# Sample rows of the attention projections as plain fp32 products on four column groups

## The chip, the cores and the metric

The kernel runs on one core of one Trainium2 chip. The metric is the device time of one execution in microseconds; the median of three runs before the change is 1368.88 us. The engines are TensorE (matrix products, PE in the rows, its weight loads PEld), VectorE (DVE), ScalarE (ACT), GpSimd (POOL) and SyncE (SP), which here only starts transfers. All run their own instruction stream and meet through semaphores.

## What is computed

Two layers of an encoder, for 512 prompt rows and 32 sample rows of width 1024. Layer 0 mixes tokens by pooling, layer 1 by banded attention with 16 heads of 64; after each comes a mixture of 32 experts of which each row uses two. The change touches one product of layer 1:

```
h   = rms_norm(x, norm_mix[1])                      # 512 + 32 rows
qkv = einsum('bld,de->ble', h, w_qkv)               # 1024 -> 3072
q   = rms_norm(qkv[:, :, 0], q_gain)                # per head
k   = rms_norm(qkv[:, :, 1], k_gain)
v   = qkv[:, :, 2]
```

The same product is taken for the prompt rows and for the sample rows.

## The kernel before

**Tiles.** The rows lie in five tiles (NT = 5): four of 128 prompt rows and one of SS = 32 sample rows. The contraction over 1024 channels goes in KT = 8 chunks of 128. The 3072 output columns go in QKV_PIECES = 6 pieces of 512: pieces 0 and 1 are q, 2 and 3 are k, 4 and 5 are v. A piece of the weights (2 MB) lies in one of the SLOTS = 3 slots of `ring`; piece j lies in slot j modulo 3. The output of tile i of piece j is bank (5 j + i) modulo 6 of PSUM.

**Split products.** A product of fp32 precision is made of three in the rounded format fp32r. ScalarE copies a quarter of a piece (two chunks) to `w_hi` rounded (line 877), VectorE takes the rest to `w_lo` (line 1268); each such copy waits on `quarters_used`, that is until TensorE has read that quarter of the piece before. The transposed rows are split likewise, `hT_hi` and `hT_lo`. `token_quarter` issues, for a prompt tile and a quarter, 2 chunks x 3 products (lines 1740 to 1742). For the sample rows `hT_sample` holds, for each chunk, 32 columns of the high part and 32 of the rest side by side, so `sample_quarter` issues 2 chunks x 2 products of 64 stationary columns (lines 2140 and 2141). Its output has 64 partitions: rows of the high part in 0 to 31 and rows of the rest in 32 to 63. ScalarE copies the upper half to `stacked` (`stack_out`, line 1118) and VectorE adds it to the lower (`add_stack`, line 1630).

**Order of a piece.** In `token_product` each of the first three quarters runs tiles 0 to 3 and then the sample rows, and then `between` transposes two finished tiles of the q or k piece before (`qk_transposes`, lines 2118 and 2120); the last quarter runs the sample rows first and then tiles 0 to 3. Each engine's order is written out by hand. ScalarE: three quarters of the next piece's split, `stack_out`, squares and roots of the five tiles (lines 1087 and 1094), or the v copies (line 1106), and then the last quarter of the split. VectorE: the same quarters, `add_stack`, head sums (line 1608), reciprocals and scalings (line 1621), last quarter. POOL multiplies by the gains (line 801) and stores k. TensorE takes a bank again when `raw_free` finds the tile six places back scaled or copied. Piece 0 has an order of its own, `first_product`, where tiles 0 to 2 run alone and tile 3 together with the sample rows.

**Around it.** SyncE loads a piece (line 683) when the piece three before is split, `split_lo`. After the last piece TensorE goes on with attention: scores (line 2241), to which VectorE adds a table of biases (line 1669) from slot 2 of the ring. POOL loads the tables (line 823) when the last piece is split, masks them (line 830), and reloads a slot when it has been read. Later the sample rows of the attention output's product run in `sample_product` (line 2309): eight fp32 products of 32 stationary columns for each half of the columns, chunk k on column group k modulo 4, and are added up by a product with `fold` (line 2316).

Of the kernel before, what the change touches and what calls it, by code (L numbers as in the profile page):

```python
# [81 lines left out]
def encoder(nc, A, O, cols):  # L82
# [32 lines left out]
    with ctx:  # L115
# [3 lines left out]
        def sem(name):  # L119
            return ctx.enter_context(nc.semaphore(name))  # L120
# [16 lines left out]
        hT_hi = nc.alloc_sbuf_tensor_at("hT_hi", [P, KT, S], F32R, offset=third_at)  # L137
        hT_lo = nc.alloc_sbuf_tensor_at("hT_lo", [P, KT, S], F32R, offset=third_at + 4 * KT * S)

        hT_sample = nc.alloc_sbuf_tensor_at("hT_sample", [P, KT, 2 * SS], F32R, offset=third_at + 8 * KT * S)  # L140
        xT_at = -(-nc.sbuf_base // 32) * 32
        xT = sb("xT", [P, 2, KT * BLK])
        hidT = sb("hidT", [P, FT * BLK])
# [129 lines left out]
        wo_all = pair[:, :, :].rearrange("p a n -> p (a n)").rearrange("p (k d) -> p k d", k=KT)  # L273
        wo_stacked = [gain[:, hf * 512:(hf + 1) * 512] for hf in range(2)]
        xT_flat = xT[:, :, :].rearrange("p u n -> p (u n)")
        stacked = xT_flat[0:SS, 0:512]
        rw_groups = xT_flat[:, 0:KT * NG]
        rw_experts = xT_flat[:, KT * NG:KT * NR].rearrange("p (g n) -> p g n", g=NG)
        early_rows = third_pair[:, 1, :]
# [105 lines left out]
        raw_ps = sem("raw_ps")  # L385
        stack_ps = sem("stack_ps")
        stack_sb = sem("stack_sb")
        sample_sum = sem("sample_sum")
        q_sq = sem("q_sq")
        q_ssq = sem("q_ssq")  # L390
# [155 lines left out]
        def _(sp):  # L546
# [32 lines left out]
            for l in range(L):  # L579
# [88 lines left out]
                if l == 0:  # L668

                    sp.wait_ge(y_ps, NEXP - 2)  # L670
                    sp.dma_start(att_gain, A["norm_mix"][1:2, :].broadcast_to((P, D))).then_inc(gain_in, 16)
                    for j in range(QKV_PIECES):
                        if j < 2:

                            sp.wait_ge(gu_ps, NEXP - 1)
                        elif j == 2:

                            sp.wait_ge(y_ps, NEXP - 1)
                        else:

                            sp.wait_ge(split_lo, QUARTERS * (j - 2))
                        to = ring[:, j % SLOTS, :].rearrange("p (k e) -> p k e", k=KT)
                        sp.dma_start(to, wqkv[:, :, j * 512:(j + 1) * 512]).then_inc(piece_in[j % SLOTS], 16)

                    half = slice(512, 1024)
                    for i in range(NT):

                        sp.wait_ge(v_sb, NT + i + 1)
                        dst = (O[5][0, 0].rearrange("t h d -> t (h d)")[i * P:(i + 1) * P, half] if i < NT - 1
                               else O[7][0, 0].rearrange("t h d -> t (h d)")[:, half])  # L690
                        sp.dma_start(dst, v_nat[0:ROWS[i], i, half]).then_inc(v_second_out, 16)
# [14 lines left out]
        def _(pool):  # L706
# [125 lines left out]
            store_first_v()  # L832

            pool.wait_ge(split_lo, QUARTERS * QKV_PIECES)
            for u in range(BIASES):
                load_bias(u)
            for u in range(BIASES):
# [15 lines left out]
        def _(act):  # L853
# [26 lines left out]
            def transpose_out(ph, i):  # L880

                n = ROWS[i]
                act.wait_ge(hT_ps, (ph - 1) * NT + i + 1)
                b = transposed_bank(ph, i)
                act.activation(hT_hi[:, :, i * P:i * P + n] if i < NT - 1 else hT_sample[:, :, 0:SS],
                               ps[:, b:b + 2, :].rearrange("p b (c t) -> p (b c) t", c=4)[:, :, 0:n],
                               ACT.Copy).then_inc(hT_hi_sb, 1)

# [220 lines left out]
            def stack_out(j):  # L1109

                if j == 0:
                    act.wait_ge(rw_set, 2)
                else:

                    act.wait_ge(sample_sum, j)
                act.wait_ge(stack_ps, j + 1)
                m = j * NT + NT - 1
                act.activation(stacked, ps[SS:2 * SS, m % RAW_BANKS, :], ACT.Copy).then_inc(stack_sb, 1)

            EARLY_HEADS = 2  # L1120

            for j in range(QKV_PIECES):
# [20 lines left out]
                if j < QKV_PIECES - 2:  # L1143
                    done = EARLY_HEADS if j == 0 else 0
                    squares(j * NT + done)
                    for i in range(done, NT):
                        if i + 1 < NT:
                            squares(j * NT + i + 1)
                        head_roots(j * NT + i)
                else:  # L1150
                    for i in range(NT):
                        v_out_of_ps((j - QKV_PIECES + 2) * NT + i)
                if j + 1 < QKV_PIECES:
                    split_att(j + 1, [QUARTERS - 1])

# [87 lines left out]
        def _(dve):  # L1243
# [27 lines left out]
            def transpose_out(ph, i):  # L1271

                n = ROWS[i]
                b = transposed_bank(ph, i)
                hi, lo = ((hT_hi[:, :, tok(i)], hT_lo[:, :, tok(i)]) if i < NT - 1 else
                          (hT_sample[:, :, 0:SS], hT_sample[:, :, SS:2 * SS]))
                dve.wait_ge(hT_hi_sb, (ph - 1) * NT + i + 1)
                V.tensor_tensor(lo, ps[:, b:b + 2, :].rearrange("p b (c t) -> p (b c) t", c=4)[:, :, 0:n],  # L1278
                                f32(hi), ALU.subtract).then_inc(hT_sb, 1)


            V.memset(spare[:, 0:1], 1.0).then_inc(spare_set, 1)
# [328 lines left out]
            def scale_heads(m):  # L1611
# [4 lines left out]
                if m >= NT:  # L1616

                    dve.wait_ge(qkT_ps, m - NT + 1)
                    if m >= 3 * NT:
# [3 lines left out]
                                bc(qstat[0:n, c + 16:c + 24], (n, 512 // HD, HD), 2),  # L1623
                                ALU.mult).then_inc(q_scaled, 1)

            def add_stack(piece):

                out = ps[0:SS, (piece * NT + NT - 1) % RAW_BANKS, :]
                dve.wait_ge(stack_sb, piece + 1)
# [4 lines left out]
            for j in range(QKV_PIECES):  # L1634

                if j == 0:
                    head_sums(0)
                    head_sums(1)
                    scale_heads(0)
                    scale_heads(1)  # L1640
                if j + 1 < QKV_PIECES:
                    split_att(j + 1, range(QUARTERS - 1))
                add_stack(j)
                if j < QKV_PIECES - 2:
                    done = EARLY_HEADS if j == 0 else 0
                    head_sums(j * NT + done)
                    for i in range(done, NT):
                        if i + 1 < NT:
                            head_sums(j * NT + i + 1)
                        scale_heads(j * NT + i)  # L1650
                if j + 1 < QKV_PIECES:
                    split_att(j + 1, [QUARTERS - 1])

# [76 lines left out]
        def _(pe):  # L1730
# [399 lines left out]
                                         w_hi[:, q, at], w_lo[:, q, at], k == 0, k == KT - 1)  # L2130
                return last

            def sample_quarter(m, q):

                for kk in range(KT // QUARTERS):
                    k = q * KT // QUARTERS + kk
                    at = slice(kk * 512, (kk + 1) * 512)
                    rows = hT_sample[:, k, :]
                    out = ps[0:2 * SS, m % RAW_BANKS, :]
                    mm(out, rows, w_hi[:, q, at], start=(k == 0), stop=False)  # L2140
                    last = mm(out, rows, w_lo[:, q, at], start=False, stop=(k == KT - 1))
                return last

            def first_product():

# [5 lines left out]
                for i in range(early):  # L2151
# [10 lines left out]
                            transposes(2, i + 2)  # L2162
                    last.then_inc(raw_ps, 1)
                sample = NT - 1
                for q in range(QUARTERS - 1):
                    if q == 0:
                        pe.wait_ge(hT_sb, NT + early + 1)
                    token_quarter(early, early, q)
                    if q == 0:
                        pe.wait_ge(z_sb[0], finished(4))  # L2170
                        pe.wait_ge(hT_sb, NT + sample + 1)
                    sample_quarter(sample, q).then_inc(quarters_used, 1)
                sample_quarter(sample, QUARTERS - 1).then_inc(stack_ps, 1)
                token_quarter(early, early, QUARTERS - 1).then_inc(quarters_used, 1)

            def token_product(piece, between):
# [3 lines left out]
                for q in range(QUARTERS - 1):  # L2180

                    pe.wait_ge(split_lo, QUARTERS * piece + q + 1)
                    for i in range(NT):
                        if q == 0:
                            raw_free(m0 + i)
                        if i < sample:
                            token_quarter(m0 + i, i, q)
                        else:
                            sample_quarter(m0 + i, q).then_inc(quarters_used, 1)
                    if between is not None:  # L2190
                        between(q)
# [120 lines left out]

            def sample_fold(hf):

                pe.wait_ge(stack_sb, QKV_PIECES + hf + 1)
# [82 lines left out]
```

## Time and profile before

| | |
|---|---|
| timed runs | 1363.88, 1368.88, 1369.61 us (median 1368.88) |
| span of the profiled execution | 1356.4 us from first to last instruction |
| the profiled execution's own time | not listed beside the three timed runs; its span is 12.5 us below their median |
| TensorE busy in the span | 1309.7 us, 97% |
| VectorE, ScalarE, POOL busy | 571.6, 299.8, 122.4 us |
| projections | 539 to 712.5 us after the span's start |

Times in the rows are microseconds from the span's start, unless marked ns. A product is shown as one record for each pass; an fp32 product leaves two, a rounded one leaves one. Products are pipelined, so a record lasts longer than the distance to the next one's start. The chain of waits goes back from the last instruction to what released each step.

### The profile page before, as it was taken

The page shows a single profiled execution, that of the slowest core. Times are in us where ns is not written, and L with a number is a line of the kernel's source. Part 1 is how long each engine was busy: PE and PEld are TensorE (multiplying, and loading weights), DVE is VectorE, ACT ScalarE, POOL GpSimd, SP SyncE. Part 2 cuts the span into 40 slices and gives each one's busy share as a digit, 9 for nine tenths or more (in the row PEclk, how much of TensorE's full clock was granted, in tenths as well). Part 3 has the DMA queues.
Part 4 walks back from the last instruction along what each step waited for, and adds up shares of the span by engine and source line. Part 5 has one row for each costly group of instructions (what it writes and reads, how often), then busy time and mean ns, then how long its engine had stood idle before and what let it go on. Part 6 is the DMA issues. An engine that isn't in the chain of part 4 may idle for free.

```text
span 1356.4 us, 19908 instructions
## 1 busy us (share of the span) xinstructions
PE 1309.7 (97%) x7552; PEld 659.5 (49%) x7552; DVE 571.6 (42%) x1057; ACT 299.8 (22%) x638; POOL 122.4 (9%) x196
## 2 busy tenths in 40 slices
PE   9999999999999999999999999999999999999998
PEld 7743344334343334788876544643344334343333
DVE  4643334333343334743418553443334433333433
ACT  4211111111111114433326443211111111111111
POOL 1010000000000001222222220010000000000000
PEclk9999999999999999999999999999999999999999
DMA  9899999999999999221038323899999999999996
GB/s 362 329 358 421 426 427 428 426 429 427 427 429 426 427 424 367 78 85 73 34 120 284 91 44 128 363 355 419 427 427 427 426 429 427 427 428 428 427 424 249
DMA packets 53504, 459.61 MB, mean 339 GB/s; under 512 B 8077, under 2 KB 9357, under 8 KB 28106
## 3 DMA queue, kind: packets, MB, share of 16 engines
q1 hardware_dynamic: 41246, 426.46, 75.3%
q0 software_dynamic: 9552, 23.94, 5.6%
q10 hardware_dynamic: 2652, 8.45, 1.7%
q8 instruction: 39, 0.64, 0.2%
q14 instruction: 15, 0.12, 0.0%
HBM read 455.42 MB, written 11.26 MB: 344 GB/s over the span
## 4 chain that ended last, share of the span: by engine, by line
PE 91%; issue 3%; DVE 3%; DMA 2%; ACT 1%; SPq 0%; POOL 0%; DVEq 0%; POOLq 0%
PE ps L1900 33%; PE ps L1931 11%; PE ps L1909 9%; PE ps L1910 8%; PE ps L2331 4%; PE ps L1740 3%; PE ps L1742 3%; PE ps L1741 3%; PE ps L1892 2%; PE ps L1824 1%; PE ps L1812 1%; PE ps L1918 1%; PE ps L2265 1%; PE ps L2281 1%; DMA ring<-in_rel_bias_reversed 1%
## 5 line engine op out<-in xcount | busy, mean ns | idle before, releaser
L1500 DVE TENSOR_TENSOR x<-x,ps 128x1024 f32<-128x1024 f32 (+1 forms) x150 | 177.7, 1216 | 222.1 <-PE ps L1931 221.0
L1900 PE MATMUL ps<-ring,xT 128*64 128x512 f32 x352 | 160.8, 606 | 8.2 <-issue 6.6
L1900 PE MATMUL ps<-pair,xT 128*64 128x512 f32 x352 | 160.7, 606 | 7.5 <-issue 7.5
L1514 DVE SCALAR_TENSOR_TENSOR nat<-nat,slot_gate,ps 64x256 f32<-64x256 f32 x128 | 86.1, 673 | 191.8 <-ACT nat L1012 163.6
L1901 PE MATMUL ps<-ring,xT 128*64 128x512 f32 x352 | 160.9, 606 | 0.0
L1901 PE MATMUL ps<-pair,xT 128*64 128x512 f32 x352 | 160.8, 607 | 0.0
L1931 PE MATMUL ps<-y_parts,hot 64*128 64x512 f32 (+1 forms) x1200 | 160.2, 401 | 0.0
L1900 PE MATMUL ps<-third_pair,xT 128*64 128x512 f32 x320 | 143.6, 597 | 7.2 <-issue 7.2
L1910 PE MATMUL ps<-qk,hidT 128*64 128x512 f32 x320 | 144.9, 595 | 0.0
L1909 PE MATMUL ps<-qk,hidT 128*64 128x512 f32 x320 | 144.7, 595 | 0.0
L1901 PE MATMUL ps<-third_pair,xT 128*64 128x512 f32 x320 | 143.8, 597 | 0.0
L1012 ACT ACTIVATE nat<-ps 64x512 f32<-64x512 f32 x62 | 36.9, 595 | 482.8 <-PE ps L1901 482.8
L1931 PEld LDWEIGHTS ps<-y_parts,hot 64*128 64x128 f32 (+1 forms) x1200 | 98.6, 171 | 71.7 <-issue 48.5
L1477 DVE TENSOR_TENSOR y_parts<-ps,y_parts 128x512 fp32r<-128x512 f32 x60 | 41.5, 692 | 133.3 <-ACT y_parts L997 133.3
L1900 PEld LDWEIGHTS ps<-ring,xT 128*64 128x64 f32 x352 | 46.3, 139 | 96.7 <-issue 95.6
L1900 PEld LDWEIGHTS ps<-pair,xT 128*64 128x64 f32 x352 | 46.2, 138 | 96.2 <-issue 95.0
L1900 PEld LDWEIGHTS ps<-third_pair,xT 128*64 128x64 f32 x320 | 41.4, 137 | 86.0 <-issue 85.0
L1909 PE MATMUL ps<-ring,hidT 128*64 128x512 f32 x176 | 79.7, 595 | 1.6 <-ACT xT L978 1.6
L1910 PE MATMUL ps<-ring,hidT 128*64 128x512 f32 x176 | 79.7, 596 | 0.0
L997 ACT ACTIVATE y_parts<-ps 128x512 fp32r<-128x512 f32 x60 | 35.8, 597 | 192.2 <-PE ps L1910 192.2
L1740 PE MATMUL ps<-w_hi,hT_hi 128*128 128x512 f32 x192 | 76.2, 397 | 0.7 <-DVE hT_lo L1278 0.7
L1742 PE MATMUL ps<-w_lo,hT_hi 128*128 128x512 f32 x192 | 74.9, 390 | 0.0
(243 smaller groups left out, 1784.4 us busy)
## 6 DMA issues: line engine op xcount, KB each, us to landing
qk<-in_moe_w_down SPq DMA_DIRECT2D x40, 2048.0 KB, 29.2
ring<-in_moe_w_down SPq DMA_DIRECT2D x22, 2048.0 KB, 26.8
ring<-in_moe_w_gate SPq DMA_DIRECT2D x20, 2048.0 KB, 24.3
ring<-in_moe_w_up SPq DMA_DIRECT2D x20, 2048.0 KB, 29.1
third_pair<-in_moe_w_gate SPq DMA_DIRECT2D x20, 2048.0 KB, 23.2
third_pair<-in_moe_w_up SPq DMA_DIRECT2D x20, 2048.0 KB, 27.9
pair<-in_moe_w_gate SPq DMA_DIRECT2D x18, 2048.0 KB, 25.9
pair<-in_moe_w_up SPq DMA_DIRECT2D x18, 2048.0 KB, 30.3
```

What stands on the lines that cost most here:

```text
L1477: V.tensor_tensor(y_rest[v], ps[:, bank, :], f32(y_high[v]), ALU.subtract).then_inc(y_lo[l], 1)
L1500: return V.tensor_tensor(x[0:n, i, :], x[0:n, i, :], ps[0:n, bank:bank + 2, :].rearrange("p b c -> p (b c)"), ALU.add)
L1514: last = V.scalar_tensor_tensor(out=out[u * BLK:(u + 1) * BLK, :].rearrange("s (k p) -> s k p", k=n), in0=act_rows[:, u * n:(u + 1) * n, : ...
L1740: mm(out, x_hi, w_h, start=start, stop=False)
L1741: mm(out, x_lo, w_h, start=False, stop=False)
L1742: return mm(out, x_hi, w_l, start=False, stop=stop)
L1900: mm(ps[BLK:P, GU_BANK, :], rows, gate[:, at], start=(k == 0), stop=(k == KT - 1))
L1901: last = mm(ps[0:BLK, GU_BANK, :], rows, up[:, at], start=(k == 0), stop=(k == KT - 1))
L1909: mm(ps[0:BLK, bank, :], rows, slot[:, at:at + 512], start=(k == 0), stop=(k == FT - 1))
L1910: last = mm(ps[BLK:P, bank, :], rows, slot[:, at + 512:at + D], start=(k == 0), stop=(k == FT - 1))
L1931: last = mm(ps[0:n, bank + hf, :], (hot[v] if by is None else by)[slots, tok(i)], part[slots, :], start=first and at == 0, stop=final and ...
L2331: last = mm(ps[:, WO_BANK, :], oT[:, k, tok(i)], wo_all[:, k, hf * 512:(hf + 1) * 512], start=(k == 0), stop=(k == KT - 1))
```

## The change

The sample rows are no longer split. `hT_sample` keeps, at the same place in memory, the transposed rows in plain fp32; ScalarE copies four chunks and VectorE the other four. For each piece `sample_rows` issues eight fp32 products of 32 stationary columns against the unsplit weights in the ring, chunk k on column group k modulo 4, so four partial sums over two chunks each lie in partitions 0 to 127 of the bank. They are added in two levels: ScalarE copies partitions 64 to 127 to `stacked_odd` and VectorE adds them to 0 to 63; then ScalarE copies 32 to 63 to `stacked` and VectorE adds them to 0 to 31.

The eight products run in one go behind the third quarter's tokens (behind the first in the last piece; between the third and the last of tile 3 in piece 0). `quarters_used` is now raised by the token products. Since the ring is read by the sample product too, SyncE's later piece loads and POOL's bias loads wait for `stack_ps` as well.

```diff
-        hT_sample = nc.alloc_sbuf_tensor_at("hT_sample", [P, KT, 2 * SS], F32R, offset=third_at + 8 * KT * S)
+        hT_sample = third_pair[:, 1, :][:, 2 * KT * S - KT * T:].rearrange("p (k t) -> p k t", k=KT)
...
-        stacked = xT_flat[0:SS, 0:512]
+        stacked_odd = xT_flat[0:2 * SS, 0:512]
+        stacked = xT_flat[0:SS, 512:1024]
...
                             sp.wait_ge(split_lo, QUARTERS * (j - 2))
+                            sp.wait_ge(stack_ps, j - 2)
...
             pool.wait_ge(split_lo, QUARTERS * QKV_PIECES)
+            pool.wait_ge(stack_ps, QKV_PIECES)
...
+                if i == NT - 1:
+                    act.activation(hT_sample[:, 0:KT // 2, 0:SS],
+                                   ps[:, b, :].rearrange("p (c t) -> p c t", c=4)[:, :, 0:n],
+                                   ACT.Copy).then_inc(hT_hi_sb, 1)
+                    return
...
                 act.wait_ge(stack_ps, j + 1)
+                m = j * NT + NT - 1
+                act.activation(stacked_odd, ps[2 * SS:P, m % RAW_BANKS, :], ACT.Copy).then_inc(stack_sb, 1)
+
+            def half_out(j):
+
+                act.wait_ge(sample_half, j + 1)
                 m = j * NT + NT - 1
                 act.activation(stacked, ps[SS:2 * SS, m % RAW_BANKS, :], ACT.Copy).then_inc(stack_sb, 1)
...
                     squares(j * NT + done)
+                    half_out(j)
...
                         v_out_of_ps((j - QKV_PIECES + 2) * NT + i)
+                        if i == 0:
+                            half_out(j)
...
+                if i == NT - 1:
+                    dve.wait_ge(hT_ps, (ph - 1) * NT + i + 1)
+                    V.tensor_copy(hT_sample[:, KT // 2:KT, 0:SS],
+                                  ps[:, b + 1, :].rearrange("p (c t) -> p c t", c=4)[:, :, 0:n]).then_inc(hT_sb, 1)
+                    return
...
+            def add_odd(piece):
+
+                out = ps[0:2 * SS, (piece * NT + NT - 1) % RAW_BANKS, :]
+                dve.wait_ge(stack_sb, 2 * piece + 1)
+                V.tensor_tensor(out, out, stacked_odd, ALU.add).then_inc(sample_half, 1)
...
-                add_stack(j)
+                add_odd(j)
                 if j < QKV_PIECES - 2:
                     done = EARLY_HEADS if j == 0 else 0
                     head_sums(j * NT + done)
+                    add_stack(j)
...
+                else:
+                    add_stack(j)
...
-            def sample_quarter(m, q):
-
-                for kk in range(KT // QUARTERS):
-                    k = q * KT // QUARTERS + kk
-                    at = slice(kk * 512, (kk + 1) * 512)
-                    rows = hT_sample[:, k, :]
-                    out = ps[0:2 * SS, m % RAW_BANKS, :]
-                    mm(out, rows, w_hi[:, q, at], start=(k == 0), stop=False)
-                    last = mm(out, rows, w_lo[:, q, at], start=False, stop=(k == KT - 1))
-                return last
+            def sample_rows(piece):
+
+                for k in range(KT):
+                    at = k % HEADS_A_GROUP * SS
+                    last = mm(ps[at:at + SS, (piece * NT + NT - 1) % RAW_BANKS, :], hT_sample[:, k, 0:SS],
+                              ring[:, piece % SLOTS, k * 512:(k + 1) * 512],
+                              start=(k < HEADS_A_GROUP), stop=(k >= KT - HEADS_A_GROUP))
+                last.then_inc(stack_ps, 1)
...
                 for q in range(QUARTERS - 1):
-                    if q == 0:
-                        pe.wait_ge(hT_sb, NT + early + 1)
-                    token_quarter(early, early, q)
-                    if q == 0:
-                        pe.wait_ge(z_sb[0], finished(4))
-                        pe.wait_ge(hT_sb, NT + sample + 1)
-                    sample_quarter(sample, q).then_inc(quarters_used, 1)
-                sample_quarter(sample, QUARTERS - 1).then_inc(stack_ps, 1)
+                    token_quarter(early, early, q).then_inc(quarters_used, 1)
+                pe.wait_ge(z_sb[0], finished(4))
+                pe.wait_ge(hT_sb, NT + sample + 1)
+                pe.wait_ge(hT_hi_sb, NT + sample + 1)
+                sample_rows(0)
                 token_quarter(early, early, QUARTERS - 1).then_inc(quarters_used, 1)
...
-                    for i in range(NT):
+                    for i in range(sample):
                         if q == 0:
                             raw_free(m0 + i)
-                        if i < sample:
-                            token_quarter(m0 + i, i, q)
-                        else:
-                            sample_quarter(m0 + i, q).then_inc(quarters_used, 1)
+                        last = token_quarter(m0 + i, i, q)
+                    last.then_inc(quarters_used, 1)
+                    if q == (0 if piece == QKV_PIECES - 1 else QUARTERS - 2):
+                        raw_free(m0 + sample)
+                        sample_rows(piece)
                     if between is not None:
                         between(q)
                 q = QUARTERS - 1
                 pe.wait_ge(split_lo, QUARTERS * piece + q + 1)
-                sample_quarter(m0 + sample, q).then_inc(stack_ps, 1)
```

## Rows read from the trace of the kernel before

**Rows 1.** The page: busy us, share of the span and records of each engine.
```profile
PE 1309.7 (97%) x7552; PEld 659.5 (49%) x7552; DVE 571.6 (42%) x1057; ACT 299.8 (22%) x638; POOL 122.4 (9%) x196
```

**Rows 2.** Stretches: start:end, length, busy us by engine, granted clock, DMA share, GB/s.
```profile
570.10:600.00 29.90, 29.90 (x152) 24.29 (x151) 13.23 (x21) 11.09 (x21) 4.92 (x4) 1.00 0.20 71
...
687.00:712.50 25.50, 25.50 (x114) 19.87 (x113) 1.91 (x2) 4.53 (x8) 6.50 (x13) 1.00 0.43 136
...
892.00:1350.00 458.00, 445.28 (x2568) 182.88 (x2570) 171.86 (x255) 65.39 (x128) 18.08 (x30) 0.99 0.98 413
```

**Rows 3.** Chain of waits, 535 to 720 us, by line.
```profile
by line: PE ps L1740 23.7%; PE ps L1742 23.4%; PE ps L1741 23.3%; PE ps L2140 6.3%; PE ps L2141 6.0%; PE ps L2118 4.9%; DMA ring<-in_rel_bias_reversed 3.7%; PE ps L2120 2.3%; PE ps L1758 2.0%; DVE hT_lo L1278 1.3%; ACT hT_hi L885 1.1%; issu
```

**Rows 4.** Waits, 535 to 720 us: who, for whom, total, times, longest.
```profile
ACT w_hi L877 <- PE ps L2141: 56.8, 15, 5.9
```

**Rows 5.** Products of line 2140: ns min/median/max, first and last start, shapes.
```profile
L2140 PE MATMUL ps<-w_hi,hT_sample x48: 387/397/443, 562.1 to 706.4; 128*64 128x512 f32 x48
```

**Rows 6.** Timeline, piece 1, second quarter: start, length, instruction.
```profile
583.30 0.39 PE L1742 MATMUL ps<-w_lo,hT_hi 128*128 128x512 f32 x1
...
583.53 0.40 PE L2140 MATMUL ps<-w_hi,hT_sample 128*64 128x512 f32 x1
...
584.45 1.95 PE L2118 MATMUL ps<-cst,nat 128*128 128x128 f32 x16
```

**Rows 7.** Chain behind 32-row transposes, piece 2.
```profile
624.07 0.37 PE ps L2140
```

**Rows 8.** Line 2309: weight loads (ns min/median/max), then timeline of products.
```profile
L2309 PEld LDWEIGHTS ps<-pair,third_pair x32: 106/110/110, 855.4 to 858.1; 128*32 128x32 f32 x32
...
855.48 3.64 PE L2309 MATMUL ps<-pair,third_pair 128*32 128x512 f32 x32 [0.87 <-DVE x L1697]
...
858.48 0.64 PE L2309 MATMUL ps<-pair,third_pair 128*32 128x512 f32 x4
...
859.05 1.16 PE L1758 MATMUL ps<-cst,third_pair 128*128 128x128 f32 x8
```

**Rows 9.** Timeline, expert stage: from rounded products into two column groups.
```profile
957.12 2.10 PE L1931 MATMUL ps<-y_parts,hot 64*128 64x512 f32 x16
959.15 0.64 PE L1900 MATMUL ps<-third_pair,xT 128*64 128x512 f32 x1
...
959.63 0.59 PE L1900 MATMUL ps<-third_pair,xT 128*64 128x512 f32 x1
```

**Rows 10.** Timeline, end of piece 0 (first row) and of piece 1.
```profile
572.09 0.69 DVE L1621 TENSOR_TENSOR nat<-ps,nat 128x512 f32<-128x512 f32 x1
...
594.71 0.39 PE L1740 MATMUL ps<-w_hi,hT_hi 128*128 128x512 f32 x1
...
594.97 0.59 ACT L1118 ACTIVATE xT<-ps 32x512 f32<-32x512 f32 x1 [0.86 <-PE ps L2141]
...
595.59 0.69 DVE L1630 TENSOR_TENSOR ps<-ps,xT 32x512 f32<-32x512 f32 x1 [0.39 <-ACT xT L1118]
...
598.29 0.69 DVE L1608 TENSOR_REDUCE nat<-nat 128x8 f32<-128x512 f32 x1 [0.68 <-ACT nat L1087]
...
601.98 0.69 DVE L1621 TENSOR_TENSOR nat<-ps,nat 128x512 f32<-128x512 f32 x1
```

**Rows 11.** Loads of the weight pieces, and ScalarE's first use of piece 3.
```profile
DMA to landing us min/median/max: 8.4/13.1/23.3
...
606.80 1.06 ACT L877 ACTIVATE w_hi<-ring 128x1024 fp32r<-128x1024 f32 x1 [2.26 <-PE ps L2141]
```

**Rows 12.** Timeline of POOL before attention.
```profile
689.72 2.18 POOL L823 DMA_DIRECT2D ring<-in_rel_bias_reversed  x3 [1.64 <-DVE w_lo L1268]
...
697.24 0.20 POOL L830 MEMSET ring<- 64x128 f32 x1 [1.06 <-DMA ring<-in_rel_bias_reversed]
```

**Rows 13.** Chain of waits where attention starts.
```profile
712.51 1.09 PE ps L2241 x8
...
715.35 6.89 DMA ring<-in_rel_bias_reversed
```

More of the change, by code:

```diff
@@ L138, in encoder @@
         hT_lo = nc.alloc_sbuf_tensor_at("hT_lo", [P, KT, S], F32R, offset=third_at + 4 * KT * S)
-        hT_sample = nc.alloc_sbuf_tensor_at("hT_sample", [P, KT, 2 * SS], F32R, offset=third_at + 8 * KT * S)
+        hT_sample = third_pair[:, 1, :][:, 2 * KT * S - KT * T:].rearrange("p (k t) -> p k t", k=KT)
+        assert hT_sample.shape[2] == 2 * SS
         xT_at = -(-nc.sbuf_base // 32) * 32
@@ L387, in encoder @@
         stack_sb = sem("stack_sb")
+        sample_half = sem("sample_half")
         sample_sum = sem("sample_sum")
@@ L884, in transpose_out @@
                 b = transposed_bank(ph, i)
-                act.activation(hT_hi[:, :, i * P:i * P + n] if i < NT - 1 else hT_sample[:, :, 0:SS],
+                if i == NT - 1:
[3 more added lines that the diff above has]
+                    return
+                act.activation(hT_hi[:, :, i * P:i * P + n],
                                ps[:, b:b + 2, :].rearrange("p b (c t) -> p (b c) t", c=4)[:, :, 0:n],
@@ L1274, in transpose_out @@
                 b = transposed_bank(ph, i)
-                hi, lo = ((hT_hi[:, :, tok(i)], hT_lo[:, :, tok(i)]) if i < NT - 1 else
-                          (hT_sample[:, :, 0:SS], hT_sample[:, :, SS:2 * SS]))
+                if i == NT - 1:
[3 more added lines that the diff above has]
+                    return
                 dve.wait_ge(hT_hi_sb, (ph - 1) * NT + i + 1)
-                V.tensor_tensor(lo, ps[:, b:b + 2, :].rearrange("p b (c t) -> p (b c) t", c=4)[:, :, 0:n],
-                                f32(hi), ALU.subtract).then_inc(hT_sb, 1)
+                V.tensor_tensor(hT_lo[:, :, tok(i)], ps[:, b:b + 2, :].rearrange("p b (c t) -> p (b c) t", c=4)[:, :, 0:n],
+                                f32(hT_hi[:, :, tok(i)]), ALU.subtract).then_inc(hT_sb, 1)
             V.memset(spare[:, 0:1], 1.0).then_inc(spare_set, 1)
@@ L1624, in scale_heads @@
                                 ALU.mult).then_inc(q_scaled, 1)
+            def add_odd(piece):
+                out = ps[0:2 * SS, (piece * NT + NT - 1) % RAW_BANKS, :]
+                dve.wait_ge(stack_sb, 2 * piece + 1)
+                V.tensor_tensor(out, out, stacked_odd, ALU.add).then_inc(sample_half, 1)
             def add_stack(piece):
                 out = ps[0:SS, (piece * NT + NT - 1) % RAW_BANKS, :]
-                dve.wait_ge(stack_sb, piece + 1)
+                dve.wait_ge(stack_sb, 2 * piece + 2)
                 V.tensor_tensor(out, out, stacked, ALU.add).then_inc(sample_sum, 1)
@@ L2164, in first_product @@
                 sample = NT - 1
+                pe.wait_ge(hT_sb, NT + early + 1)
                 for q in range(QUARTERS - 1):
-                    if q == 0:
-                        pe.wait_ge(hT_sb, NT + early + 1)
-                    token_quarter(early, early, q)
-                    if q == 0:
-                        pe.wait_ge(z_sb[0], finished(4))
-                        pe.wait_ge(hT_sb, NT + sample + 1)
-                    sample_quarter(sample, q).then_inc(quarters_used, 1)
-                sample_quarter(sample, QUARTERS - 1).then_inc(stack_ps, 1)
+                    token_quarter(early, early, q).then_inc(quarters_used, 1)
[3 more added lines that the diff above has]
+                sample_rows(0)
                 token_quarter(early, early, QUARTERS - 1).then_inc(quarters_used, 1)
@@ L2313, in sample_fold @@
             def sample_fold(hf):
-                pe.wait_ge(stack_sb, QKV_PIECES + hf + 1)
+                pe.wait_ge(stack_sb, 2 * QKV_PIECES + hf + 1)
                 mm(ps[0:SS, WO_SAMPLE_BANKS[hf], :], const("fold"), wo_stacked[hf], start=True,
```

## The prediction

> **What bounds the kernel now.** I read the page's busy shares and slices first. TensorE is busy 97% of the span, VectorE 42%, ScalarE 22% [rows 1]. The change lies between the two expert stages, so the next views are of that part. Seen by stretches, the projections run from 539 to 712.5 us, and from 562.1 us on TensorE is busy in all of each stretch, 29.90 of 29.90 us in piece 1 and 25.50 of 25.50 in piece 5 (first and last of five stretches alike), at clock 1.00, which is the level of 2.4 GHz, while the DMA share is 0.20 and 0.43 [rows 2]. The chain of waits over 535 to 720 us runs through TensorE products nearly throughout, and the sample rows' two lines hold 6.3% and 6.0% of it, 22.8 us of 185 [rows 3]. ScalarE waited 56.8 us there for the last sample product of a quarter [rows 4]: it follows TensorE with room, and VectorE follows it. So a microsecond taken from TensorE in this stage comes off the end, as long as no wait takes its place.
>
> **What is removed.** Sixteen rounded products per piece (8 chunks by two weight parts), 96 in all: 48 on line 2140 [rows 5] and as many on 2141. Each lasts about 0.40 us but the next starts 0.23 us later: four from 583.53, and the following transposes start at 584.45, 0.92 us for four [rows 6]. 96 x 0.23 = 22.1 us. The chain's 22.8 us holds in addition a first product of 0.37 instead of 0.23 us behind each block of 32-row transposes [rows 7]. In the new order a token product stands there and should pay the same 0.14 us (five times 0.7 us), so I don't count it.
>
> **What is added on TensorE.** Eight fp32 products of 32 columns per piece, 48 in all. The same pattern is already in the kernel: the attention output's sample rows (line 2309) run sixteen such products, each of which leaves two records, 32 in all [rows 8]. They start at 855.48 us, the last four records start together at 858.48, and the next work starts at 859.05. Eight waves of four: seven intervals in 3.00 us, 0.43 us each. A piece needs 8 products x 2 records / 4 = 4 waves, 4 x 0.43 = 1.71 us. Two costs come with it. Leaving the groups: 859.05 - 858.48 = 0.57 us instead of 0.43, so 0.14. Entering them from a full stream of products: line 2309 starts after a wait and can't show it. The nearest rows are the expert stage, where 16 rounded products on two halves of the array (8 pairs, at 0.23 us 1.84 us) start at 957.12 and two column groups start at 959.15, 2.03 us later, with 0.48 us to the next pair instead of 0.43 [rows 9]: 0.19 + 0.05 = 0.24 at most. The switch from full width to 64 columns at 583.53 costs nothing [rows 6]. I take 0.2, nearer to the group case. So 1.71 + 0.14 + 0.2 = 2.05 us a piece, 12.3 us for six.
> The bounds: no switching cost, 1.71 x 6 = 10.3 us; at the other end four weight loads of 0.11 us (the median of line 2309's loads is 110 ns) one after the other before the groups run, 0.44 + 0.05 + 0.14 + 1.71 = 2.34 us, 14.0 us for six [rows 8, 9].
> The Trainium skill, "TensorE: Matmul & The Clock Gate", Part 3, "Measured speedup vs the span model", gives 3.07x for four tiles packed by rows and 2.38x for three by columns, not the full 4x and 3x. By 3.07x, eight products that take 6.83 us in sequence would take 2.22 us, six pieces 13.3 us, and the gain would be 8.8 us; the waves of 0.43 us in line 2309 don't show that loss, but its ends might be where it sits.
>
> **Sum.** 22.1 - 12.3 = 9.8 us less TensorE work on the path; by the bounds 22.1 - 14.0 = 8.1 to 22.1 - 10.3 = 11.8.
>
> **The longer addition.** Each piece now needs two evictions and two additions for the sample rows instead of one of each. ScalarE gains a copy of 0.6 us and VectorE an addition of 0.7 us per piece (over 32 partitions they take 0.59 and 0.69 us, and VectorE takes the same 0.69 over 128, so I give 64 partitions the same) [rows 10]. In 29.90 us of a piece VectorE is busy 13.23 and ScalarE 11.09 us [rows 2]: throughput is no matter. Order is. Queued behind the first new addition on VectorE are the head sums and scalings; TensorE's next piece waits for them before it reuses a bank. Tile 3's first quarter in the next piece needs tile 2 scaled. Piece 1's last quarter starts at 594.71 and holds 24 products, so it ends at about 600.2, and tile 3 is due three tiles (18 products, 4.1 us) later, 604.3; tile 2's scaling starts at 601.98 and lasts 0.69: 1.6 us of room [rows 10]. The first addition falls before the last quarter, since the sample product moves ahead of it, and its transposes and 5.5 us of tokens cover it. The second falls between two head sums where VectorE waited 0.68 us for ScalarE [rows 10], and it is 0.69 long: about 0.1 us later, hidden. In piece 0 the products 2 and 3 come closer: tile 2's scaling ends at 572.8 [rows 10] and is due 4.1 us behind 570.1, at 574.2 [rows 2]; both move up by some 2 us, the scaling perhaps by 0.4 us less, still 0.8 us of room. If that cover went, each addition would cost up to its 0.7 us, in five pieces 3.5 us. The copies of the sample's transposed rows were 0.38 us on ScalarE and then 0.42 on VectorE, and now run beside each other; TensorE wasn't waiting for them, so nothing.
>
> **The new waits.** SyncE may load piece j only after sample product j-3. Piece 3's load, before released by the split of piece 0, now goes at about 567 (570.1, where piece 0's products ended, less the 1.4 us of its last quarter and the 1.6 us gained); piece 4's at about 590, piece 5's near 618. The longest such load took 23.3 us to land [rows 11]. ScalarE took piece 3 up behind piece 2's first quarter, at 606.80 [rows 11], so now at about 603.5, and pieces 4 and 5 one piece of about 28 us later each: 13 us of room or more. Behind the wait in SyncE's queue are only the later pieces and then the second value half's stores, which wait for later work anyway. POOL's bias loads wait for the last sample product. They were issued at 689.72, 22.8 us ahead of the end of the projections, and their last mask was written at 697.24, 7.5 us later [rows 12]. The last piece does its sample product after its first quarter, 5.5 + 2.05 us from its start, and the piece lasts 25.5 - 1.6 us: the loads go 16.4 us ahead of the end and are ready 8.9 us ahead. The cached values and four sample tables queued behind them end 3 us later. Hidden; without the cover, each microsecond would delay the first scores.
>
> **What follows.** Attention starts right behind the last projection product: scores at 712.51, then VectorE, then a bias load of 6.89 us that is issued only once a slot is read [rows 13]. All of it, and layer 1's expert loads, are released by progress, not by a clock, so 9.8 us move to the end: span 1356.4 -> 1346.6. The runs' median is 1368.88, 12.5 us above this span; I take that distance as fixed: 1368.9 - 9.8 = 1359.1 us.
>
> **The rivals.**
> (a) The sum holds, 8.1 to 11.8 us gained, 1357.1 to 1360.8. For it: TensorE without a gap in the stage. Chance 0.67.
> (b) More is lost at the edges of the groups, or the additions make the next piece wait by their 0.7 us: gain 9.8 - 3.5 = 6.3, or down to 3 with both, 1362 to 1366. Against it: the room worked out above; for it: 0.8 us in piece 0 is thin and the entry isn't shown. Chance 0.17.
> (c) The gain is spent at the border to attention: the bias loads go 16.4 instead of 22.8 us ahead and would have to take over 16 us (7.5 shown), or layer 1's transfers, at a DMA share of 0.98 in its stage [rows 2], don't start sooner. The loads start on attention's progress, which speaks against it. Gain under 3 us, 1366 to 1370. Chance 0.06.
> (d) Slower: products that read the raw weights from the ring while ScalarE, VectorE and DMA use it don't run four at a time. In sequence a piece costs 16 x 0.43 = 6.8 us instead of 3.68, six pieces 18.9 us more: 1387.8. It decides from the point where fewer than 1.9 groups run at once. Line 2309 speaks against it. Chance 0.03.
> (e) More than the sum: entries cost nothing and the 0.14 us after the transposes goes too, gain 12 to 14 us, 1355 to 1357. Chance 0.07.
>
> **Numbers.** A measurement of this kernel tells about 0.5% (6.8 us) from no change: faster than 1362.0. (a) and (e) and a third of (b), with something off for the scatter of runs (1363.88 to 1369.61 before), give 0.77 faster; (c) and most of (b) 0.18 the same; (d) and mishaps 0.05 slower. The range reaches over (e) and into (b): 1354 to 1364.5.
>
> **What the changed profile would show.** TensorE still busy in every stretch of the projections; 96 records on the new sample line, 16 a piece within about 1.9 us of starts, in waves of four 0.43 us apart; no wait of a token product for VectorE's scaling or for the split weights; scores starting some 9.8 us sooner and everything after at the old distances. Records that start one by one would prove (d); a TensorE wait for the scaling (b); a late first bias mask (c).

## The result, and the profile after

The changed kernel took 1351.97 us (median of four executions, 1349.69 to 1354.55), beside 1366.38 us (1360.69 to 1369.61) for the kernel before: ratio 0.9898, 95% interval 0.9876 to 0.9920. The forecast was 1359.1 us, 1354.0 to 1364.5: faster, as forecast, but 14.4 us instead of 9.8, and below the range. Two later sets with more executions, each with both kernels on one chip, put the ratio at 0.9925 (0.9899 to 0.9950) and 0.9930 (0.9904 to 0.9956), with medians of 1353.43 against 1363.01 us and 1353.20 against 1361.88. One of the changed kernel's 22 executions in the three sets fell in a slow state and took 2608.72 us, at a mean granted clock of 1.00; why is not known, and it is left out of every figure here.

The page's first line answers to [rows 1]:

```profile
PE 1302.5 (96%) x7552; PEld 651.2 (48%) x7552; DVE 577.8 (43%) x1063; ACT 303.7 (22%) x644; POOL 122.8 (9%) x196
```

TensorE gave up 7.2 us of busy time, VectorE and ScalarE took on 6 instructions each. The next fence has the changed kernel in stretches, as [rows 2] but for TensorE alone: start:end, length, busy us and records, granted clock, DMA share, GB/s. The borders are the same events in each kernel: the first expert transposes, the first projection product, the first scores, the first sample product of line 2309 (2336 after), layer 1's first gathered transposes, the end.

```profile
74.20:540.30 466.10, 451.10 (x2603) 0.99 1.00 420
540.30:704.90 164.60, 163.49 (x832) 0.99 0.24 81
704.90:848.50 143.60, 135.82 (x941) 1.00 0.44 138
848.50:895.00 46.50, 44.81 (x279) 1.00 0.94 377
895.00:1351.30 456.30, 438.58 (x2515) 0.99 0.97 411
```

The same borders in the kernel before, first profile:

```profile
74.70:539.10 464.40, 450.57 (x2603) 0.99 1.01 421
539.10:712.40 173.30, 172.23 (x832) 1.00 0.23 78
712.40:855.50 143.10, 135.89 (x945) 1.00 0.44 138
855.50:901.90 46.40, 44.78 (x279) 1.00 0.94 377
901.90:1356.40 454.50, 437.37 (x2515) 0.99 0.98 413
```

Read down the lengths: the projections went from 173.3 to 164.6 us, and the other stretches differ by 0.1 to 1.8 us, all against the changed kernel. The spans are only 5.1 us apart while the timed medians are 14.4 apart. The changed kernel's profiled execution took 1353.18 us at a span of 1351.3, 1.9 us more than its span; with that, the profile of before belongs to an execution of about 1358.3 us, below all four timed ones and 8 us below their median of 1366.38. And the 164.6 us hold something that isn't the change, in this fence of 4 us stretches of the changed kernel:

```profile
556.00:560.00 4.00, 2.93 (x20) 1.00 0.00 0
560.00:564.00 4.00, 4.00 (x14) 0.59 0.45 131
564.00:568.00 4.00, 4.00 (x21) 0.99 0.00 0
```

TensorE had waited 1.1 us for the rest of tile 3's rows (busy 2.93 of 4.00), then the granted clock fell to its lower level of 1.2 GHz for part of 560 to 564 us: 4 x 0.41 = 1.6 us of work lost, which leaves 163.0 us. The kernel before has the same wait at the same place and did not lose its clock there in either profile.

The new products, in piece 0 and in piece 2 (timeline of the changed kernel; line 2168 is `sample_rows`, 1771 to 1773 the token products, 2149 the transposes):

```profile
567.45 0.39 PE L1773 MATMUL ps<-w_lo,hT_hi 128*128 128x512 f32 x1
567.77 1.92 PE L2168 MATMUL ps<-ring,third_pair 128*32 128x512 f32 x16
569.62 0.50 PE L1771 MATMUL ps<-w_hi,hT_hi 128*128 128x512 f32 x1
569.96 0.40 PE L1772 MATMUL ps<-w_hi,hT_lo 128*128 128x512 f32 x1
...
619.29 0.39 PE L1773 MATMUL ps<-w_lo,hT_hi 128*128 128x512 f32 x1
619.61 1.92 PE L2168 MATMUL ps<-ring,third_pair 128*32 128x512 f32 x16
621.46 1.07 PE L2149 MATMUL ps<-cst,nat 32*128 32x32 f32 x8
622.46 0.50 PE L1771 MATMUL ps<-w_hi,hT_hi 128*128 128x512 f32 x1
622.80 0.40 PE L1772 MATMUL ps<-w_hi,hT_lo 128*128 128x512 f32 x1
```

Sixteen records from 567.77 to the next start at 569.62, 1.85 us. Entering costs 0.32 instead of 0.23 us, and the first token product behind holds 0.34 instead of 0.23: in all 1.85 + 0.09 + 0.11 = 2.05 us, the value of the sum [rows 8, 9]. In pieces 1 to 4 32-row transposes follow, and the kernel before already paid for entering those. The same place there, in piece 2:

```profile
622.67 0.40 PE L2141 MATMUL ps<-w_lo,hT_sample 128*64 128x512 f32 x1
623.00 1.07 PE L2118 MATMUL ps<-cst,nat 32*128 32x32 f32 x8
624.00 0.44 PE L2140 MATMUL ps<-w_hi,hT_sample 128*64 128x512 f32 x1
624.28 0.40 PE L2141 MATMUL ps<-w_lo,hT_sample 128*64 128x512 f32 x1
```

The entry cost 0.33 us before and costs 0.32 now, and the product behind the transposes holds 0.34 us instead of 0.28. So these pieces pay 1.85 + 0.06 = 1.91 us.

The longer addition, in piece 0 (timeline of ScalarE and VectorE, answering to [rows 10]):

```profile
569.82 0.60 ACT L1128 ACTIVATE xT<-ps 64x512 f32<-64x512 f32 x1 [0.82 <-PE ps L2168]
570.45 0.69 DVE L1652 TENSOR_TENSOR ps<-ps,xT 64x512 f32<-64x512 f32 x1 [0.19 <-ACT xT L1128]
571.17 0.59 ACT L1134 ACTIVATE xT<-ps 32x512 f32<-32x512 f32 x1
571.79 0.69 DVE L1658 TENSOR_TENSOR ps<-ps,xT 32x512 f32<-32x512 f32 x1
573.25 0.69 DVE L1643 TENSOR_TENSOR nat<-ps,nat 128x512 f32<-128x512 f32 x1
```

The 64-partition forms took 0.60 and 0.69 us, as set. Tile 2's scaling, which stands behind both additions on VectorE, starts at 573.25, and no token product waited for it. POOL's bias loads (answering to [rows 12]) went at 689.05, released by the sample product, 16 us ahead of the first scores at 704.9, and the third mask was written at 696.29:

```profile
689.05 2.19 POOL L827 DMA_DIRECT2D ring<-in_rel_bias_reversed  x3 [6.85 <-PE ps L2168]
696.29 0.20 POOL L834 MEMSET ring<- 64x128 f32 x1 [1.10 <-DMA ring<-in_rel_bias_reversed]
```

### The profile page after: what moved, and what is told of

Same layout as the page of the kernel before. It is cut to its first block, busy times and chain, and to the rows that moved or that the text cites. A ratio compares the mean times of both kernels' runs of the same rounds, so it can differ in the third digit from the quotient of the medians.

```text
span 1351.3 us, 19924 instructions
## 1 busy us (share of the span) xinstructions
PE 1302.5 (96%) x7552; PEld 651.2 (48%) x7552; DVE 577.8 (43%) x1063; ACT 303.7 (22%) x644; POOL 122.8 (9%) x196
## 4 chain that ended last, share of the span: by engine, by line
PE 88%; DMA 5%; issue 3%; DVE 2%; ACT 1%; SPq 0%; POOL 0%; POOLq 0%; DVEq 0%
PE ps L1931 32%; PE ps L1962 11%; PE ps L1940 8%; PE ps L1941 8%; PE ps L2358 4%; PE ps L1771 3%; PE ps L1772 3%; PE ps L1773 3%; DMA ring<-in_rel_bias_reversed 2%; PE ps L1923 2%; DMA ring<-in_attn_w_qkv 1%; PE ps L1855 1%; PE ps L1843 1%; PE ps L1949 1%; PE ps L1789 1%
## 5 line engine op out<-in xcount | busy, mean ns | idle before, releaser
L1931 PE MATMUL ps<-third_pair,xT 128*64 128x512 f32 x320 | 145.3, 602 | 7.8 <-issue 7.8
L1932 PE MATMUL ps<-third_pair,xT 128*64 128x512 f32 x320 | 145.4, 603 | 0.0
L1772 PE MATMUL ps<-w_hi,hT_lo 128*128 128x512 f32 x192 | 75.6, 394 | 0.0
```

The source lines that it names most:

```text
L1772: mm(out, x_lo, w_h, start=False, stop=False)
L1931: mm(ps[BLK:P, GU_BANK, :], rows, gate[:, at], start=(k == 0), stop=(k == KT - 1))
L1932: last = mm(ps[0:BLK, GU_BANK, :], rows, up[:, at], start=(k == 0), stop=(k == KT - 1))
```

## The experiments

All of them start from the kernel before or the changed one. Where a kernel has a single execution, only the length of its stretches is used, since one execution's time says little here.

**The kernel before against itself.** No edit.

> The kernel before, unchanged, against itself. Its first profile had a span of 1356.4 us, while its timed runs lie at 1360.7 to 1369.6; the changed kernel's profiled run took 1353.18 us at a span of 1351.3, 1.9 us apart. Theory A (the change is worth what the projections lose, 8.7 to 10 us, and the rest of the measured 14.4 us is scatter of the kernel before): ratio 1.000 within 0.003, and single executions spread over some 5 to 10 us, with the spread in the expert stages or the granted clock and the projections at 173.3 us from their first product to the first scores (539.1 to 712.4) as in the first profile. Theory B (the change gains another 4 to 5 us outside the projections): the kernel before lies steadily near 1366 us, and a second profile shows some stretch outside the projections longer than in the changed kernel.

Measured: 1364.34 us over 12 executions (1358.81 to 1370.51) against 1363.01 us over 29 (1357.28 to 1373.13), ratio 1.000 (0.9974 to 1.0025). Its profile:

```profile
540.40:713.80 173.40, 172.33 (x834) 1.00 0.23 78
713.80:857.20 143.40, 135.79 (x941) 1.00 0.43 138
```

The projections repeat to 0.1 us. The executions don't: they spread over 16 us, wider than the 5 to 10 expected, and the time follows the mean granted clock of each: over this kernel's 58 executions here and in the last set the standard deviation is 3.5 us, and 1.7 us around a straight line in the clock. Execution and clock, a few from this set: 1358.81 us at 0.996, 1361.71 at 0.993, 1365.05 at 0.991, 1367.64 at 0.988, 1370.51 at 0.987; among the other 29, the three at 0.986 took 1370.56 to 1373.13. Both of theory A's numbers came: ratio 1.000, and 173.4 us.

**The changed kernel again, twice.** No edit.

> The changed kernel once more, five rounds. Theory A: 9 to 10 us faster than before, ratio 0.993 (0.991 to 0.995). Theory B: 14 to 15 us faster, ratio 0.9895. In the profile both expect the projections at 163 to 165 us from their first product to the first scores.

Measured: 1353.43 us over 11 executions, ratio 0.9925 (0.9899 to 0.9950), medians 9.6 us apart. The profile, without a dip of the clock in the stage:

```profile
541.70:704.70 163.00, 161.93 (x834) 1.00 0.24 82
704.70:849.10 144.40, 135.79 (x941) 1.00 0.43 137
```

> The changed kernel a third time, five more rounds, since single executions spread by 10 us and more. If the change is worth what the stage lost (173.4 to 163.0 us, 10.4 us), the ratio over these runs lies at 0.9925 within 0.002 whatever the draw of the kernel before; if the first measurement's 14.4 us were real, at 0.9895. Where the granted clock of an execution is higher, its time should be lower by about 1.1 us per 0.001.

Measured: 1353.20 us (1350.61 to 1354.73, 6 executions), ratio 0.9930 (0.9904 to 0.9956), projections again 163.0 us (540.4 to 703.4). So the stage lost 173.4 - 163.0 = 10.4 us, and theory A's numbers stand: 0.9895, theory B's ratio, lies outside both intervals. A straight line fitted through 103 single executions of five kernels (one constant for each kernel, one slope for the clock) gives 1.08 us per 0.001 of mean clock with 1.8 us left over, and the changed kernel 10.7 us faster than before at equal clock (9.8 to 11.6).

**The sample products twice.**

```diff
-                for k in range(KT):
+                for k in list(range(KT)) * 2:
```

> The changed kernel with each piece's eight sample products issued twice in a row, the second time starting the sums anew, so the values stay as they were. It prices the pass over four groups: 4 more waves a piece of 0.43 us, 1.7 to 1.8 us, six pieces 10.3 to 10.8 us, no further entry or exit. Theory A: 10.3 to 10.8 us slower than the changed kernel, ratio to before 1.000 to 1.001 (if the changed kernel is at 0.993). Theory B, where time off or onto TensorE in this stage comes out about 1.4 times as large at the end (14.4 / 10): 14 to 15 us slower than the changed kernel. A serial pass would cost 41 us.

Measured: 1362.40 us over ten executions, ratio to before 0.9989 (0.9963 to 1.0014); 9.0 us above the changed kernel's 1353.43 and 10.7 us above it at equal clock. The stage:

```profile
543.10:716.40 173.30, 172.23 (x930) 1.00 0.22 78
```

173.3 - 163.0 = 10.3 us for 24 more waves, 0.43 us each. Time put onto TensorE here comes out at the end as it goes in; theory B's factor of 1.4, which asks for 14 to 15 us, is refuted.

**Half of the removed products.** In the kernel before:

```diff
-                    mm(out, rows, w_hi[:, q, at], start=(k == 0), stop=False)
-                    last = mm(out, rows, w_lo[:, q, at], start=False, stop=(k == KT - 1))
+                    last = mm(out, rows, w_hi[:, q, at], start=(k == 0), stop=(k == KT - 1))
```

> The kernel before without the sample rows' products against the rest of the weights (line 2141; the low part of the weights is left out for the sample rows): 48 rounded products fewer and nothing else. Theory A: 48 x 0.23 = 11.0 us faster, ratio 0.992. Theory B, 1.4 times: 15 to 16 us, ratio 0.989.

Measured: 1349.40 us, ratio 0.9893 (0.9843 to 0.9944) over four executions; 12.2 us at equal clock, within 1.8. The plain ratio allows both theories; at equal clock 11.0 us lies within and theory B's 15 to 16 outside. The stage shows what the removed products were worth there:

```profile
538.00:700.40 162.40, 161.33 (x785) 1.00 0.24 84
```

173.4 - 162.4 = 11.0 us, 48 x 0.23, to the tenth.

**Two groups and one group.** In the changed kernel, with 2, then 1, in place of the four:

```diff
-                    at = k % HEADS_A_GROUP * SS
+                    at = k % 2 * SS
...
-                              start=(k < HEADS_A_GROUP), stop=(k >= KT - HEADS_A_GROUP))
+                              start=(k < 2), stop=(k >= KT - 2))
```

> The changed kernel with the eight sample products on two column groups instead of four (the two levels of addition are left in place and add stale partitions, so the sample rows' values are not those of the reference). If the groups run at once, as the sum has it, a piece needs 8 waves instead of 4, 4 x 0.43 = 1.7 us more, six pieces 10.3 us: the projections (first product to first scores, 163.0 us in an execution with no dip of the clock in them) at 173.3 us. If the gain came mainly from taking plain fp32 products and not from the groups, the stage would stay at 163 to 165 us.

> The same on one column group: all eight products in one sum over the chunks, so nothing can overlap (the two levels of addition again add stale partitions). 16 passes of 0.43 us, 6.8 us a piece, 12 passes or 5.1 us more than with four groups, six pieces 30.7 us: projections at 163.0 + 30.7 = 193.7 us, less the switching. This is the rival in which the change would be slower, made on purpose: 20 us over the kernel before. The other theory, that the records on one group hide behind each other as the rounded ones do, would give 173 to 180 us.

Measured, two groups and then one:

```profile
540.40:713.60 173.20, 172.13 (x832) 1.00 0.22 77
```

```profile
544.30:739.70 195.40, 194.32 (x832) 0.99 0.20 70
```

173.2 us as expected, and 195.4 us, of which a stretch at the lower clock (564 to 572 us) took 1.7, so 193.7. From the first record of a sample product to the next work it is 1.85, 3.55 and 6.98 us for four, two and one groups. The gain hangs on the four groups: on two groups plain fp32 gives nothing over the kernel before, on one it is the slower rival (d), 20 us worse.

**The bias loads released late.**

```diff
-                    if q == (0 if piece == QKV_PIECES - 1 else QUARTERS - 2):
+                    if q == QUARTERS - 2:
```

> The changed kernel with the last piece's sample product behind its third quarter instead of its first, so that the loads of the bias tables are released some 5.5 us ahead of the first scores instead of 16.4. The prediction's reading: 7.5 us are needed from the issue of the first load to the last mask of three, so the third table is some 2 us late; attention's first units wait, and from the first scores to the sample rows of the output product (143.1 to 144.4 us in five executions) it takes 1 to 3 us longer. The rival: the first two tables suffice, since the fourth table's 6.9 us of landing stands in the chain anyway, and nothing changes; the projections stay at 163 us under both.

> The changed kernel with the last piece's sample product behind its third quarter, timed. Its first profile showed attention 9 us longer than in the changed kernel, with TensorE idle for 7.8 us and the clock at half level right after. If the late release of the bias loads is the cause and not a chance of that execution: 7 to 10 us slower than the changed kernel, ratio to before 0.998 to 1.000, and the same idle time in the new profile. If it was chance: ratio 0.9925 as the changed kernel.

Measured, in the first profile: attention from the first scores to the sample rows' product took 153.0 us instead of 143.6 to 144.4, far more than 1 to 3 us. POOL's timeline, the two places that waited on it (one line of VectorE, one of TensorE) and TensorE's stretches show how:

```profile
700.63 2.19 POOL L827 DMA_DIRECT2D ring<-in_rel_bias_reversed  x3 [17.73 <-PE ps L2168]
710.64 2.20 POOL L846 DMA_DIRECT2D ring<-in_rel_bias_reversed  x4
712.83 1.43 POOL L827 DMA_DIRECT2D ring<-in_rel_bias_reversed  x2
721.55 0.20 POOL L834 MEMSET ring<- 64x128 f32 x1 [7.29 <-DMA ring<-in_rel_bias_reversed]
721.78 0.69 DVE L1700 CUSTOM_DVE_ANT_0 ring<-ps,ring 128x512 f32<-128x512 f32 x1 [8.09 <-POOL ring L834]
724.78 1.94 PE L2292 MATMUL ps<-cst,ring 128*128 128x128 f32 x8 [7.85 <-DVE ring L1720]
```

```profile
716.00:720.00 4.00, 0.94 (x8) 0.95 1.03 286
720.00:724.00 4.00, 0.00 (x0) 0.50 0.94 347
724.00:728.00 4.00, 3.22 (x22) 0.50 0.69 222
728.00:732.00 4.00, 4.00 (x36) 0.77 0.50 151
```

The loads went 5.0 us ahead of the first scores at 705.6, and the three tables themselves came in time for the first units. But the cached values and the four sample tables stand behind the third mask in POOL's queue and now went at 710 us. The fourth table, which the next unit needs, was issued behind them at 712.83, 7.2 us after the first scores instead of 2.9, and its mask came 8.7 us later, where it took 6.9 to 7.3 otherwise; in the second profile it took 10.3. TensorE waited 7.8 us, and the clock then stood at the lower level until past 728 us. Timed: 1361.21 us, ratio 0.9992 (0.9973 to 1.0011), 8.0 us slower than the changed kernel; the second profile has 154.2 us and a wait of 9.4. The cause is the late release, not chance, and it eats four fifths of the gain. At equal clock it is 5.1 us slower by the straight line above, so some 3 of the 8 us came by the lower clock.

**The addition made longer.** In the changed kernel, ahead of the first copy and the first addition, two more of each (the second hunk is VectorE's):

```diff
+                for half in range(2):
+                    act.activation(xT_flat[2 * SS:P, half * 512:(half + 1) * 512], ps[2 * SS:P, m % RAW_BANKS, :], ACT.Copy)
                 act.activation(stacked_odd, ps[2 * SS:P, m % RAW_BANKS, :], ACT.Copy).then_inc(stack_sb, 1)
...
+                for half in range(2):
+                    V.tensor_copy(xT_flat[2 * SS:P, half * 512:(half + 1) * 512], ps[2 * SS:P, (piece * NT + NT - 1) % RAW_BANKS, :])
                 V.tensor_tensor(out, out, stacked_odd, ALU.add).then_inc(sample_half, 1)
```

> The changed kernel with two more copies on ScalarE and two more on VectorE in front of the first level of each piece's addition, 1.2 and 1.4 us, into memory that nobody reads. It prices the cover of the longer addition. By the prediction's room (0.8 us in piece 0, 1.5 us or more in the others, and the chain partly covered by the last quarter): the projections at 163.0 to 165 us, with a wait of TensorE's token product in piece 1 for VectorE's scaling of at most 1 us. If the addition were a hidden part of the path, six times 2.6 us would come on top, 178 us.

Measured:

```profile
541.40:708.20 166.80, 164.70 (x832) 0.99 0.24 80
```

Of the 166.8 us 1.7 is a stretch at the lower clock (560 to 568 us), which leaves 165.1, 2.1 us more than 163.0. TensorE waited at tile 3 in piece 1, where the prediction had it:

```profile
576.08 0.39 PE L1777 MATMUL ps<-w_lo,hT_hi 128*128 128x512 f32 x1
577.47 0.50 PE L1775 MATMUL ps<-w_hi,hT_hi 128*128 128x512 f32 x1 [1.00 <-DVE nat L1645]
```

577.47 - 576.08 is 1.39 us where 0.23 is usual: 1.2 us late, a little over the 1 us expected, out of 2.6 us of added work. The room in piece 0 is therefore about 1.4 us. From one sample product to the next, three later pieces got 0.3 us longer each, so by the same subtraction their room is about 2.3 us.

## Why the prediction was right and wrong

**The terms on TensorE were right.** Removed: 22.1 us; half of it, removed alone, was 11.0 us. Added: 2.05 us a piece was exact where tokens stand on both sides (pieces 0 and 5), and it was 1.91 us in pieces 1 to 4, since the sum charged there for an entry which the transposes had cost before as well. 2 x 2.05 + 4 x 1.91 = 11.7 us instead of 12.3, a gain of 10.4, and the stage shows 10.4. One group against four is 6.98 / 1.85 = 3.8x, and the doubled products cost 0.43 us a wave: the waves of line 2309 were the right guide. The Trainium skill ("TensorE: Matmul & The Clock Gate", Part 3) measured 3.07x for four row tiles; this kernel's column groups do better than that. Three small sums of the prediction don't come out of its own numbers, and none of them moved the 1359.1 us: the 32-row transposes stand in four pieces, so 4 x 0.14 = 0.6 us and not "five times 0.7 us"; the room in piece 0 is 1.4 - 0.4 = 1.0 us and not 0.8; and rival (e) reaches at most 11.8 + 0.6 = 12.4 us of gain and not 14.

**The rivals.** (b) did not happen: no token product waited, the room in piece 0 was about 1.4 us and not 0.8, and with another 2.6 us of work put in front TensorE waited 1.2 us. (c) did not either, but the prediction sized it wrong. It took the three masks, 7.5 us, as the need and the queue behind them as a matter of "3 us later"; the runs with the late release show that exactly that queue decides, and that an advance of 5.0 us instead of 16 costs 8 us. (d) is refuted by the 1.85 us for sixteen records and by the runs with fewer groups. A small part of (c) may be there: attention took 143.6, 144.4 and 144.2 us in the changed kernel's three profiles against 143.1 and 143.4 before, but 143.5, 143.7 (145.4 less a stretch at the lower clock), 142.8 and 143.1 in the four variants of it with the same release (products twice, two groups, one group, longer addition), so it isn't settled whether 0.5 to 1 us is the change's. Together 10.4 less that fits the 9.6 us between the medians of the larger set and the 8.7 of the smaller.

**What failed** is the step "I take that distance as fixed: 1368.9 - 9.8 = 1359.1 us", and with it the range and what it was taken to hold. Of the 12.5 us between the span and the median only 1.9 us stand around every span. The rest was the difference between one execution that kept its clock (mean 0.995) and a median of three that most likely had not: their clocks aren't on record, but by the straight line a time of 1368.9 belongs to a clock near 0.987. Over 58 executions the kernel before has a median of 1363.0 us, and 1363.0 - 9.8 = 1353.2, which is the changed kernel's median over 21 executions (1353.18). That this agrees to 0.1 us is luck in part, since the stage lost 10.4 and attention may have given some of it back. And 1353.2 lies below the stated range of 1354.0 to 1364.5 as well. The first measurement's 14.4 us came from four executions of before whose median lay 3.4 us above that, and four of the changed kernel 1.2 us below theirs. The range of 1354 to 1364.5 was built from the rivals' costs alone, where the scatter of single executions, 1357 to 1373 us in the kernel before, is wider than the whole range. The chance for (e), more than the sum, was not the place of it: nothing in the kernel gained 14 us.

Where the scatter comes from is shown, what triggers it is not. The profiles have stretches of half clock, each worth about 1.7 us: three or four in the profiles of before, three to six in those of the changed kernel. Most stand in the expert stages behind a wait of TensorE; in the first profile of before:

```profile
360.00:364.00 4.00, 1.62 (x10) 0.85 1.02 434
364.00:368.00 4.00, 4.00 (x16) 0.72 0.99 422
```

TensorE waited 2.3 us at 421 to 424 us in both profiles of the kernel before, and the clock fell behind that wait in the first and not in the second. So a wait alone doesn't decide it, and what does stays open.

## What to carry to other kernels

Price a change from the stage's length between two fixed events in profiles without a clock dip, which repeated here to 0.1 us, and expect the end-to-end time to move by that, but start the absolute forecast from the median of many executions and give it their scatter: neither the median of three, 1368.9 us, nor the 1358.3 us that belong to the profile was the 1363.0 us of 58. Stationary tiles of 32 columns on four column groups run nearly four at a time (1.85, 3.55 and 6.98 us for four, two and one), and fp32 in plain form then beat the split into rounded products for these 32 rows; on two groups the two were even, so count the groups that you can fill before you drop the split. When a load may go only after a product has read the buffer, place the product by everything that is queued behind that load: here moving eight products by two quarters cost 8 us.

## What the runs showed of the hardware

The mean granted clock of one core alone ran from 0.986 to 0.996 between executions of the kernel before, and 0.001 of it was worth 1.08 us of 1363. A switch from full-width products to four column groups cost 0.09 us going in, and going out 1.85 - 4 x 0.43 = 0.13 us plus 0.11 us in the product behind. Behind a wait of 7.8 us the lower clock level stayed until about 5 us after TensorE had work again at 724.78: granted clock 0.50 from 720 to 728 us, and 0.77 from 728 to 732.
